# A two-layer diffusion block on one core: global heads turned before the Fourier products, modulation steps one place earlier, the extra weight slot from the first expert's head

## The reference

```python
h = modulate(rms_norm(x, norm1_g[l]), sh1, sc1)          # 256 latent tokens, width 1024
hc = modulate(rms_norm(xc, norm1_g[l]), csh1, csc1)      # 256 context tokens
y, yc = mixer_sublayer(h, hc, ...)     # in-projection, three branches, gates, out-projection
x = x + g1 * y
x = x + g2 * expert_choice_ffn(modulate(rms_norm(x, norm2_g[l]), sh2, sc2), ...)
```

## Time and profile before

| | |
|---|---|
| time, median of 3 runs (lowest, highest) | 2332.78 us (2329.54, 2335.97) |
| profiled execution: its time, its span | 2328.48 us, 2326.7 us |
| PE busy (matmuls) | 2030.6 us, 87% |
| DVE, ACT busy | 670.7 us, 431.0 us |
| read from memory | 595.71 MB |
| granted PE clock, mean | 0.938 of full |

### The profile page before, as it was taken

How to read it: one execution, slowest core, us unless ns; L and a number is a source line. 1 busy time by engine, 2 the same in 40 slices (tenths; PEclk the granted TensorE clock), 3 DMA queues, 4 the chain that set the end, 5 groups by cost and what they waited for, 6 DMA issues and landing times.

```text
span 2326.7 us, 21571 instructions
## 1 busy us (share of the span) xinstructions
PE 2030.6 (87%) x8606; PEld 1000.7 (43%) x8606; DVE 670.7 (29%) x1613; ACT 431.0 (19%) x888; POOL 0.2 (0%) x4
## 2 busy tenths in 40 slices
PE   6989899999988988898899978788776688979998
PEld 3445444445432333233554433333221255748863
DVE  2266210125112222123551142122210158730001
ACT  3045200014100000002150022103100032530000
POOL 0000000000000000000000000000000000000000
PEclk9999999999998999899999989999897899989999
DMA  9129721311699999996275557999999963132432
GB/s 367 73 86 360 269 89 56 117 72 73 266 430 428 428 429 428 427 426 241 91 294 185 172 217 313 425 419 425 429 428 429 430 237 109 37 108 98 156 136 81
DMA packets 111614, 598.15 MB, mean 257 GB/s; under 512 B 9255, under 2 KB 15223, under 8 KB 86811
## 3 DMA queue, kind: packets, MB, share of 16 engines
q1 hardware_dynamic: 107920, 591.82, 63.2%
q10 hardware_dynamic: 3595, 4.95, 0.6%
HBM read 595.71 MB, written 1.05 MB: 256 GB/s over the span
## 4 chain that ended last, share of the span: by engine, by line
PE 70%; DMA 21%; DVE 5%; ACT 2%; issue 2%; SPq 0%; DVEq 0%; ACTq 0%
PE bank L1285 24%; DMA weight_ring<-in_w_up_e 12%; PE bank L1686 10%; PE bank L637 7%; PE bank L1713 4%; PE bank L656 3%; PE bank L1669 3%; DMA weight_ring<-in_w_down_e 3%; PE bank L1234 3%; DMA weight_ring<-in_w_ada 3%; DMA arena<-in_w_up_e 2%; PE bank L1251 2%; PE bank L1524 2%; PE bank L434 2%; PE bank L1458 2%
## 5 line engine op out<-in xcount | busy, mean ns | idle before, releaser
L1285 PE MATMUL bank<-weight_ring,arena 128*128 128x512 f32 (+1 forms) x1328 | 560.4, 584 | 3.7 <-DMA weight_ring<-in_w_in 1.7
L1285 PEld LDWEIGHTS bank<-weight_ring,arena 128*128 128x128 f32 x1328 | 252.1, 190 | 307.5 <-issue 298.1
L1686 PE MATMUL bank<-weight_ring,arena 128*64 128x512 f32 x832 | 250.9, 641 | 45.7 <-DMA weight_ring<-in_w_up_e 27.6
L1669 PE MATMUL bank<-weight_ring,arena 128*32 128x512 f32 x816 | 146.7, 745 | 68.7 <-DMA weight_ring<-in_w_up_e 54.1
L1713 PE MATMUL bank<-weight_ring,arena 128*64 128x512 f32 (+1 forms) x816 | 184.8, 598 | 20.6 <-DMA weight_ring<-in_w_down_e 16.4
L3062 ACT ACTIVATE arena<-bank 64x512 f32<-64x512 f32 (+1 forms) x64 | 37.7, 589 | 638.6 <-PE bank L1686 411.1
L637 PE MATMUL bank<-arena,weight_ring 128*128 128x256 f32 x704 | 155.2, 384 | 0.8 <-DVE small L2312 0.8
L1686 PEld LDWEIGHTS bank<-weight_ring,arena 128*64 128x64 f32 x832 | 78.7, 148 | 171.3 <-issue 167.6
L1234 PE MATMUL bank<-const,arena 128*128 128x128 f32 (+3 forms) x764 | 108.4, 291 | 42.5 <-DVE arena L2155 10.2
L637 PEld LDWEIGHTS bank<-arena,weight_ring 128*128 128x128 f32 x704 | 135.8, 193 | 20.2 <-issue 1.1
L1234 PEld LDWEIGHTS bank<-const,arena 128*128 128x128 f32 (+3 forms) x764 | 93.5, 169 | 94.5 <-issue 76.0
(11 more groups left out here) (386 smaller groups left out, 1826.6 us busy)
## 6 DMA issues: line engine op xcount, KB each, us to landing
weight_ring<-in_w_up_e SPq DMA_DIRECT2D x52, 2048.0 KB, 14.7
weight_ring<-in_w_gate_e SPq DMA_DIRECT2D x51, 2048.0 KB, 16.2
weight_ring<-in_w_down_e SPq DMA_DIRECT2D x51, 2048.0 KB, 13.7
weight_ring<-in_w_in SPq DMA_DIRECT2D x25, 2048.0 KB, 10.9
weight_ring<-in_w_ada SPq DMA_DIRECT2D x24, 2048.0 KB, 11.9
arena<-in_w_gate_e SPq DMA_DIRECT2D x13, 2048.0 KB, 15.6
arena<-in_w_down_e SPq DMA_DIRECT2D x13, 2048.0 KB, 15.3
arena<-in_w_up_e SPq DMA_DIRECT2D x12, 2048.0 KB, 16.3
```

The source lines that it names most:

```text
L1285: mm = pe.matmul(b[:, 0:c1 - c0], lhs[:, k, t * P:t * P + P], slot_view(r)[:, k, c0:c1], start=(k == 0), stop=(k == ks - 1))
L1669: mm = pe.matmul(b[c:c + R, :], xgT[1][:, KH * half + k, e, :], wide(r)[:, k, n * 512:n * 512 + 512], start=(half == 0 and k == 0), stop=( ...
L1686: mm = pe.matmul(banks_[n][c:c + R, :], xgT[l][:, KH * half + k, e, 0:R], wide(r)[:, k, n * 512:n * 512 + 512], start=(half == 0 and k == ...
```

## The change

It has four parts. (1) The global keys and queries are turned as soon as DVE has rotated them, before the Fourier products, and only the window heads are turned after the scores of the first two groups have been issued; four transposes share a bank where it was two before. (2) Each modulation step's key is one lower, and the first now stands at -1, between the scores of the first two groups and the turning of the window heads; layer 0 has none at 3 and 11 now (before: none at 4, and at 11 only a turning). (3) In layer 0, `pick` and `pick_g` move to another place and become one buffer; the extra slot takes the fifth expert load instead of the seventh, and waits for `m_ready`, a signal from the middle of the mixer. (4) In layer 0's `experts` the affinities are turned before the last three gatherings of the latent stream; the turning of the picks and the spreading of the second gate move from before the gatherings to behind `turn_hidden(0)`, with their copies on ACT, and the weighting of the picks on DVE to behind the gathering. In layer 1 only the turning of the picks moves, to behind `gate_up(0, 1)`.

```diff
-    first = {0: ((0, 2), None), 1: ((0, 3), None), 2: ((0, 4), (0, 3)), 3: ((0, 5), (0, 4)), 5: ((1, 0), None), 6: ((1, 1), (1, 0)),
-             7: ((1, 2), (1, 1)), 8: ((1, 3), None), 9: ((1, 4), (1, 3)), 10: ((1, 5), None), 11: (None, (1, 4))}
-    second = {0: ((2, 0), None), 1: ((2, 1), (2, 0)), 2: ((2, 2), (2, 1)), 3: ((2, 3), None), 4: ((2, 4), (2, 3)), 5: ((2, 5), (2, 4))}
+    first = {-1: ((0, 2), None), 0: ((0, 3), None), 1: ((0, 4), (0, 3)), 2: ((0, 5), (0, 4)), 4: ((1, 0), None), 5: ((1, 1), (1, 0)),
+             6: ((1, 2), (1, 1)), 7: ((1, 3), None), 8: ((1, 4), (1, 3)), 9: ((1, 5), None), 10: (None, (1, 4))}
+    second = {-1: ((2, 0), None), 0: ((2, 1), (2, 0)), 1: ((2, 2), (2, 1)), 2: ((2, 3), None), 3: ((2, 4), (2, 3)), 4: ((2, 5), (2, 4))}
...
-        pick = (area(12288, TILES, 512), area(10240, 2, 512))
-        pick_g = (area(14336, TILES, 512), area(11264, 2, 512))
+        pick = [[area(at, 512) for at in tiles] for tiles in ((19456, 19968, 18432, 18944), (10240, 10752))]
+        pick_g = (pick[0], [area(at, 512) for at in (11264, 11776)])
...
+                pe.wait_ge(S("rope_global_ready"), due("rope_global_ready"))
+                turn_keys(GK)
+                for t in own:
+                    turn_queries((t,), GQ, 4, "DA"[t // 2])
...
-                pe.wait_ge(S("z_ready_act"), due("z_ready_act"))
-                pe.wait_ge(S("rope_ready"), due("rope_ready"))
-                for t in tiles:
-                    turn_k(t)
-                for t in own:
-                    turn_q(t, "DA"[t // 2])
...
-                if l:
-                    extra_free[1, RING] = ("m_ready", 2)
+                extra_free[l, RING] = ("m_ready", l + 1)
...
+            def turn_queries(tiles, c0, pairs, pool):
+
+                b = bank(pool)
+                for i, t in enumerate(tiles):
                     for j in range(pairs):
-                        mm = turn(b[:, j * P:j * P + P], Z[:, t, c0 + j * P:c0 + j * P + P])
-                    mm.then_inc(S("full" + pool), 1)
-
-            def turn_k(t):
-                pe.wait_ge(S("freeA"), due("freeA"))
-                b = bank_of("A", T.n["freeA"])
-                turn(b[:, 0:P], Z[:, t, GK:GK + P])
-                turn(b[:, P:2 * P], Z[:, t, WK:WK + P]).then_inc(S("fullA"), 1)
+                        at = (i * pairs + j) * P
+                        mm = turn(b[:, at:at + P], Z[:, t, c0 + j * P:c0 + j * P + P])
+                mm.then_inc(S("full" + pool), 1)
...
+            def turn_keys(c0):
+
+                b = bank("A")
+                for t in range(TILES):
+                    mm = turn(b[:, t * P:t * P + P], Z[:, t, c0:c0 + P])
+                mm.then_inc(S("fullA"), 1)
...
+                if -1 in LATE_STEPS[l]:
+                    mod_step(*LATE_STEPS[l][-1])
+                pe.wait_ge(S("z_ready_act"), due("z_ready_act"))
+                pe.wait_ge(S("rope_ready"), due("rope_ready"))
+                turn_keys(WK)
+                turn_queries((0, 1), WQ, 2, "D")
+                if streams == 2:
+                    turn_queries((2, 3), WQ, 2, "A")
+                window_dve, window_act = T.n["freeD"], T.n["freeA"]
...
+                    if step == 0:
+                        pe.wait_ge(S("freeD"), POOL + window_dve)
+                        pe.wait_ge(S("freeA"), POOL + window_act)
...
+                turn_aff(last, bank("D"))
                 gather_first(range(5, 8))
-                turn_aff(last, bank("D"))
-                broadcast_gate2(l, ns)
-                if l == 0:
-                    turn_picks(0, 0, "A")
+                if l:
+                    broadcast_gate2(l, ns)
...
-                slots.add(RING, 4 if l else 6)
+                slots.add(RING, 4)
...
-                turn_picks(l, last, "A")
-                put_copied = T.n["freeA"]
-                if l == 0:
-                    extra_free[0, RING] = ("fullA", put_copied)
+                gathered_jobs[l] = high_act
                 pe.wait_ge(S("freeD"), POOL + late_job)
                 pe.wait_ge(S("freeA"), POOL + high_act)
                 gate_up(0, 1, pair)
+                if l:
+                    turn_picks(l, last, "A")
+                    put_copied[l] = T.n["freeA"]
                 for e in range(E):
                     turned = next_bank()
                     if e + 1 < E:
                         pair = next_pair(e + 1)
                         gate_up(e + 1, 0, pair)
                     turn_hidden(e, turned)
+                    if l == 0 and e == 0:
+                        turn_picks(0, 0, "A")
+                        turn_picks(0, 1, "A")
+                        put_copied[0] = T.n["freeA"]
+                        broadcast_gate2(0, 2)
...
+                dve.memset(flag, 0.0).then_inc(S("rope_global_ready"), 1)
+                dve.wait_ge(S("rope_global_ready"), due("rope_global_ready"))
                 take_z(2)
+                rope(0, WQ, 6)
+                for t in range(2):
+                    take_global_queries(t)
                 take_fourier()
                 dve.wait_ge(S("z_ready_act_v"), due("z_ready_act_v"))
-                for t in range(2):
-                    rope(t, WQ, 6)
+                rope(1, WQ, 6)
...
                     if step - 1 in LATE_STEPS[l]:
                         mod_step(*LATE_STEPS[l][step - 1])
+                    if step == 0:
+                        take_window_queries()
...
                 start_tile(2 * last + 1)
-                if l == 0:
-                    weigh_picks(0, 0)
                 take_logit_parts(last)
...
+                if l == 0:
+                    dve.wait_ge(S("fullA"), gathered_jobs[0])
+                    weigh_picks(0, 0)
+                    weigh_picks(0, 1)
...
+                take_keys(1)
+                if streams == 2:
+                    take_queries(2, 2, 4, 2)
...
+                take_keys(0)
+                for t in own[2:]:
+                    take_queries(t, 1, 0, 4)
...
+                scale_rows(last)
                 if l == 0:
                     take_gathered(l, 0, range(5, 8))
-                scale_rows(last)
...
+                    if l == 0 and e == 0:
+                        take_picks(0)
+                        take_picks(1)
+                        take_gate2()
```

81 lines of the change are left out of this document (40 added, 41 removed).

## The result

The changed kernel takes 2317.7 us (median of 6, 2314.0 to 2322.4), the kernel before 2333.1 beside it: ratio 0.9933, 95% interval 0.9919 to 0.9947. The gain is 15.4 us; the forecast was 2313 and a gain of 19.4, so the time lies inside the range. The profiled execution took 2318.7, span 2316.9.

A forecast was written before the change was run, and what follows sets the result against it. PE was taken to bound the mixers and the weight DMA the two sets of experts. Terms 6.9 + 10.4 + 2.7 - 0.6 = 19.4 took the profiled 2328.5 to 2309.1; forecast median 2313 us, range 2304 to 2325.

The forecast's parts named there:

- Start of attention, layer 0: Layer 0's mixer: with global heads turned early, first scores come at 141.7, a gain of 2.5 us (bounds 1.5 and 4.5).
- The softmax gap, layer 0: PE's 4.89 us idle before the first weighted probabilities takes a modulation product and 12 transposes; 4.9 us leave the path.
- the layer's 6.9 in all: Layer 0's mixer: 2.5 + 4.9 - 0.5 - 1.0 + 1.0 = 6.9 us gained.
- the new bare step at the end: Layer 0's attention: moving the modulation steps leaves a new bare step at 11, costing 1.0 us.
- Rival (b): Attention is paced by DVE, ACT and the weights, not PE; only earlier starts count: 11.1 gained, 2321.7 us, chance 0.22.
- The wait for weights: Layer 0's modulation steps: a product's wait of 3.62 us shrinks to about 2.5, 1.0 gained (bounds 0 and 4.9).
- Layer 1: Layer 1's mixer: scores 6.5 us sooner, 4.6 of work into the gap, minus 0.7 for ACT's copies: 10.4 gained.
- Router: Context stream's affinities turned at once instead of after three gatherings; everything behind is 2.7 us sooner.
- clock in the gathering: Router's gathering: the clock can stay up, 2.6 us more gained, or fall as before; nothing counted.
- Extra slot: Layer 0's experts: the saved 4.9 us load is eaten by dry spells, net -0.6 us (bounds -4 and +4.9).
- both dry spells: Layer 0's experts: the DMA runs dry for 3.7 and 1.8 us, before the releases at 13.5 and 34.9.
- The clock, rival (d): The granted clock falls in each of 18 attention steps, costing 27 us: slower, 2340 us, chance 0.03.

The follow-up runs named there:

- half_loads: Changed kernel, loading only the first half of the rows of weights for layer 1's six modulation products (does not compute the reference): 2308.7 us.
- aff_late: Changed kernel, but the context stream's affinities are turned behind the last three gatherings again, as before: 2319.4 us.
- no_bare_step: Changed kernel, but layer 0's ten products stand at steps -1 to 8 without a gap, steps 10 and 11 bare: 2313.6 us.
- experts_only: Kernel before with the experts' part of the change alone (affinities early, picks and gate moved, extra slot at the head): 2333.4 us, ratio 1.0005.
- picks_behind: Changed kernel, but in layer 0 the turning of the picks and spreading of the gate stand behind gate_up(1, 1): 2309.3 us.
- both: Changed kernel with the edits of no_bare_step and picks_behind in one: 2311.6 us.
- two_ahead: The version both, with two modulation products, (0,2) and (0,3), in layer 0's softmax gap and all others one step earlier: 2311.5 us.
- six_and_behind: Changed kernel with the edit of picks_behind, and layer 0's extra slot joining at the seventh load again: 2313.4 us.
- mixers_only: Kernel before with the mixers' part of the change alone; router, picks and extra slot as before: 2316.5 us, ratio 0.9926.

## Why the prediction was right, and where it was wrong

- **Start of attention, layer 0: 2.5 forecast, 3.3 measured.** Right; DVE's wait inside the Fourier products vanished altogether.
- **The softmax gap, layer 0: 4.9, and the layer's 6.9 in all.** This is the step that failed: the claim that work taken off PE leaves the path to the end of the attention. I summed PE's work as if it set the pace to the end. It does up to the first of the six products, and there the gain arrives: 83.5 from P0 before, 74.7 after, 8.8 less, when the clock falls twice. From there the loads set the pace, 48.3 to 48.9 us in all traces but three (half_loads; aff_late with its falls; no_bare_step with 49.1), and behind the last product now stand two steps, 12.6 instead of 8.6. I had charged 1.0 for the new bare step at the end; it costs 4. So 4.9 remain with two clock falls, and -0.3 with four, which eat 5.3 (the changed kernel's own two traces both have four). Rival (b) had this for layer 0, but by way of the weights alone, as half_loads shows.
- **The wait for weights: 1.0 of gain.** 3.30 instead of 3.62, but 1.97 instead of 0.39 on the product before; no gain. The release some 15 us sooner was spent at the bare step, where all slots were full.
- **Layer 1: 10.4 forecast, 13.1 measured in the pair, the same in every trace with the early heads and this table.** Start 6.5 against 7.0. The rest is larger by 2.2, as the low clock behind the idle gap went too: the 16 transposes at 1163.89 took 3.65, where now 24 transposes take 3.06 (2.40 and 0.66), and the eight records of scores behind them take 1.99 instead of 2.95.
- **Router: 2.7 against 3.1 to 3.7** (3.3 in the pair), 2.3 of chain and 0.9 to 1.0 of clock in the gathering, which I had left at zero between 0 and 2.6.
- **Extra slot: -0.6.** The places of both dry spells were right to 0.4 us; their sizes were 3.1 and 0.5 instead of 3.7 and 1.8. With these the sum would be a gain of 1.3 (4.9 - 3.1 - 0.5), yet the stage lost 0.5 to 3.1 in seven traces (mean 451.7 against 450.3): the saved load does not bring its 4.9. Mis-sized was also what follows: another 1 to 4 us of clock in the stretch to P1, so 3.4 in all on the mean. It swallows the router's gain, which is why experts_only gives nothing. That the second dry spell belongs to this loss is shown by five versions that have the changed router and not this spell, and lose nothing; how a pause of 0.5 us at 638 makes the clock fall at 1057 is not.
- **The clock, rival (d)**: it did not decide, but it took part of what was gained, 5.3 us in layer 0's attention in half of the eight traces with its code. In these traces the clock falls while PE is busy (0.50 at 179 to 181, above). The Trainium skill's page "TensorE: Matmul & The Clock Gate", section "A second HAM failure mode: psum-queue depth-cycling", has the clock swing when PE idles briefly between groups of matmuls; that small idle times bring the falls about is not shown here.

The forecast was 4.7 too low because 6.9 and -0.6 were 4.9 or less and -3.4, and layer 1 paid 2.8 back. If half of the executions have two falls in layer 0 and half four, the terms add up to 2.3 + 13.1 + 3.2 - 3.4 = 15.2, and the medians differ by 15.4. So near an agreement is partly luck: that share is a guess from eight traces, and that the time lies inside the range also owes something to the 2.8 us of layer 1, which I had not seen. The versions that mend the experts' part (picks_behind, both, two_ahead, six_and_behind) have medians of 2309.3 to 2313.4, 4 to 8 under the changed kernel. picks_behind, 2309.3, is the lowest of those that compute the whole reference; its interval overlaps the others' and that of the changed kernel.

## What to carry to other kernels

Filling an idle gap pays only up to the next place that another engine paces: find the last stretch before the stage's end, ask what paces it, and count what stands behind its last item. When a ring of slots is full, an earlier release is worth nothing until the consumer takes from it; a step without a consumer is a pause of the DMA. And when a combined change gives less than its parts, run the parts alone: the loss here sat in a stretch that no edit touched.

## What was not expected of the hardware

PE's clock went to 1.2 GHz for 3 to 4 us at a time while PE was busy in the whole of each window, and the same instructions had it in one execution and not in the next (the 16 transposes above: 0.50 and 3.45 us, 1.00 and 1.97 us). In a stretch that the DMA paces this cost nothing: with 3.4 us of work lost to it in mixers_only and 1.8 in the changed kernel (the sum of 1 minus PEclk over windows of 1 us), the six products took 48.4 and 48.3 us. That holds only up to a point: in aff_late 7.2 were lost, and they took 51.9. In a stretch that PE paces it costs all of it and more: 6.8 instead of 3.4 lost made 80.0 out of 74.7, and 1.4 of these 5.3 us are a longer wait for ACT (2.12 ahead of the product with the values at 205.68, against 0.68 at 198.95 in picks_behind).
